# Attention scores over four rotating PSUM banks, and a ring of three banks for everything else

## What is computed

```python
s = (jnp.einsum('bqhd,bkhd->bhqk', qn_b, k_nope)
     + jnp.einsum('bqhr,bkr->bhqk', qr_b, k_rope)) * ATTN_SCALE
p = jax.nn.softmax(s.astype(jnp.float32), axis=-1).astype(v.dtype)
return jnp.einsum('bhqk,bkhd->bqhd', p, v)
```

## Time and profile before

| | |
|---|---|
| median of three executions | 1463.22 us (1460.0 to 1464.26) |
| the profiled execution | 1462.78 us |
| its span | 1460.6 us |
| TensorE busy in the span | 1377.5 us (94%) |
| attention, first score to the closing stage's first data | 183.7 to 514 us |

### The profile page before, as it was taken

How to read it: one execution, slowest core, us unless ns; L and a number is a source line. 1 busy time by engine, 2 the same in 40 slices (tenths; PEclk the granted TensorE clock), 3 DMA queues, 4 the chain that set the end, 5 groups by cost and what they waited for, 6 DMA issues and landing times.

```text
span 1460.6 us, 20549 instructions
## 1 busy us (share of the span) xinstructions
PE 1377.5 (94%) x7548; PEld 1236.6 (85%) x7548; DVE 818.7 (56%) x1206; ACT 708.7 (49%) x1416; POOL 441.9 (30%) x542
## 2 busy tenths in 40 slices
PE   5899889999999979999999999999999999999996
PEld 1599878999888858899999888899998879999995
DVE  6577577777777744245555455544445545444444
ACT  5677567787777732243333443433334433333332
POOL 3476637888778624450000001100000020000002
PEclk9899999999999989999999999999999999999999
DMA  8522001111111060053443333433333334333321
GB/s 295 168 77 78 28 17 40 42 42 42 42 37 37 25 243 1 34 219 137 160 170 129 116 115 116 159 142 115 128 130 116 116 116 159 142 115 129 130 86 43
DMA packets 50445, 154.63 MB, mean 106 GB/s; under 512 B 9832, under 2 KB 12392, under 8 KB 50376
## 3 DMA queue, kind: packets, MB, share of 16 engines
q1 hardware_dynamic: 49512, 150.60, 29.3%
q0 software_dynamic: 864, 3.15, 0.5%
HBM read 148.73 MB, written 4.83 MB: 105 GB/s over the span
## 4 chain that ended last, share of the span: by engine, by line
PE 60%; DVE 2%; POOL 1%; ACT 1%; DMA 0%; issue 0%; DVEq 0%; ACTq 0%; POOLq 0%
PE bank L2048 27%; PE bank L2040 26%; PE bank L1756 6%; POOL x L1829 1%; PE bank L1530 1%; DVE wol L1718 0%; DMA add<-in_w_o 0%; DVE w1l L1935 0%; DVE w2l L1935 0%; PE bank L1561 0%; DVE add L1979 0%; PE bank L2062 0%; ACT w2h L1866 0%; DVE rTl L1946 0%; ACT rTh L1884 0%
## 5 line engine op out<-in xcount | busy, mean ns | idle before, releaser
L2040 PE MATMUL bank<-h2h,w1l 128*128 128x384 f32 x768 | 258.2, 336 | 0.0
L2040 PE MATMUL bank<-h2l,w1h 128*128 128x384 f32 x768 | 258.2, 336 | 0.0
L2040 PE MATMUL bank<-h2h,w1h 128*128 128x384 f32 x768 | 258.2, 336 | 0.0
L1829 POOL TENSOR_TENSOR x<-x,add 128x512 f32<-128x512 f32 x16 | 20.9, 1334 | 717.8 <-DVE add L1979 717.8
L2048 PE MATMUL bank<-w2h,rTh 128*128 128x512 f32 x576 | 182.7, 398 | 7.8 <-DVE rTl L1946 7.8
L2048 PE MATMUL bank<-w2l,rTh 128*128 128x512 f32 x576 | 179.7, 393 | 0.0
L2048 PE MATMUL bank<-w2h,rTl 128*128 128x512 f32 x576 | 179.0, 392 | 0.0
L1884 ACT ACTIVATE rTh<-sq 128x384 fp32r<-128x384 f32 x94 | 49.4, 525 | 243.6 <-PE bank L2048 239.7
L1873 ACT ACTIVATE relu<-bank 128x384 f32<-128x384 f32 x94 | 46.1, 491 | 247.1 <-PE bank L2040 247.1
L1946 DVE TENSOR_TENSOR rTl<-sq,rTh 128x384 fp32r<-128x384 f32 x96 | 53.6, 558 | 174.1 <-ACT rTh L1884 169.9
L1935 DVE TENSOR_TENSOR w1l<-w1raw,w1h 128x1024 fp32r<-128x1024 f32 x94 | 117.2, 1247 | 55.2 <-ACT w1h L1866 55.2
(11 more groups left out here) (269 smaller groups left out, 2904.2 us busy)
## 6 DMA issues: line engine op xcount, KB each, us to landing
w1raw<-in_w SPq DMA_DIRECT2D x96, 512.0 KB, 3.7
w2raw<-in_w SPq DMA_DIRECT2D x96, 512.0 KB, 4.6
ada_raw<-in_w_ada SPq DMA_DIRECT2D x24, 512.0 KB, 4.8
xn<-in_w_ada SPq DMA_DIRECT2D x16, 512.0 KB, 3.5
xin<-in_x SPq DMA_DIRECT2D x9, 512.0 KB, 3.6
x<-in_x SPq DMA_DIRECT2D x3, 1536.0 KB, 12.4
g_raw<-in_w_ada SPq DMA_DIRECT2D x8, 512.0 KB, 3.5
out_y<-x POOLq DMA_DIRECT2D x6, 512.0 KB, 5.4
```

The lines of the kernel that those rows point to most:

```text
L1829: nc.gpsimd.tensor_tensor(k.x[:, t, cut], k.x[:, t, cut], add[:, i, :], ALU.add).then_inc(out_added, 1)
L2040: op = nc.tensor.matmul(bank[6 + s][:, 0:BN], w[0][s][x][:, c * P:(c + 1) * P], k.h2[b % 2][y_][:, c, :], start=n == 0, stop=n == 3 * DC - 1)
```

## The change

The scores get a fourth bank: column c of unit u is item n = 3u + c and goes to bank n % 4 of banks 0 to 3. It waits for the exponential that read item n-4. An access can't wrap from bank 3 to bank 0, so the unit's three columns are read as 2 and 1, and in units with u % 4 = 1 (columns in banks 3, 0, 1) as 1 and 2. The ring loses bank 3: item n waits for the reader of item n-3. Side products move: keys from x = 0, 3, 5 to 1, 3, 6, queries from 1, 4, 7 to 2, 5, 7. On VectorE `low_key` moves from behind `maximum(u)` to the head of the unit, ahead of the output sum and the maximum. The gate columns of unit 0 go through bank 3, and the wait for their reader moves to the start of `scores(1)`.

The items that a side or context product waits for, by unit of a head (T2 same unit means: the low half of this unit's own T2):

| x | before: item and what it waits for | after |
|---|---|---|
| 0 | k0: q2 | |
| 1 | q0: k0 | k0: T2 same unit |
| 2 | | q0: k0 |
| 3 | k1: T1 of u-1; context: T2 same unit | k1: T2 same unit; context: T3 same unit; T4: q0 |
| 4 | q1: k1 | T1: k1 |
| 5 | k2: q1; context: T2 same unit | q1: T2 same unit; context: T3 same unit |
| 6 | | T1: q1; k2: context of u-1 |
| 7 | q2: T1 of u-1; context: T2 same unit | T4: k2; q2: T2 same unit; context: T3 same unit |

```diff
--- before.py
+++ after.py
@@ -318,7 +318,7 @@
         LAST = NU + 4
         NV = LT + 2
         KCUT = ((0, 512), (512, 1024), (1024, NKEY))
-        SIDE_AT = {0: ("k", 0), 1: ("q", 0), 3: ("k", 1), 4: ("q", 1), 5: ("k", 2), 7: ("q", 2)}
+        SIDE_AT = {1: ("k", 0), 2: ("q", 0), 3: ("k", 1), 5: ("q", 1), 6: ("k", 2), 7: ("q", 2)}
         NADA = 16
         ADA0 = 3 * DC
         ADA_AT = {4 + 15 * r // 4: r for r in range(NADA)}
@@ -328,7 +328,18 @@
         KEY_ITEM, QUERY_ITEM = (2, 3, 4), (1, 5, 6)
         VALUES_FREE = {2: 6 + NV - 1, 3: 6 + NV}
         VALUES_AT = {0: range(0, 2), 1: range(2, 6), 2: range(6, NV)}
-        scores_in, pv_bank, ring_banks = k.banks[:, 0:3, 0:BN], bank[6], (bank[3], bank[4], bank[5], bank[7])
+        pv_bank, ring_banks = bank[6], (bank[4], bank[5], bank[7])
+
+        def score_parts(u):
+
+            first = 3 * u % 4
+            cut = 1 if first == 3 else 2
+            return [(first + lo) % 4 for lo in (0, cut)], ((0, cut), (cut, 3))
+
+        def score_read(n):
+
+            u, c = divmod(n, 3)
+            return 2 * u + 1 + (c >= score_parts(u)[1][0][1])
 
         def query(n, x):
 
@@ -380,11 +391,11 @@
         place = {item: n for n, item in enumerate(ring)}
 
         def ring_bank(what, i):
-            return ring_banks[place[what, i] % 4]
+            return ring_banks[place[what, i] % 3]
 
         def ring_free(pe, what, i):
 
-            n = place[what, i] - 4
+            n = place[what, i] - 3
             if n < 0:
                 return
             kind, j = ring[n]
@@ -826,8 +837,8 @@
                         act.wait_ge(rs_ready, 2 * u - 14)
                     if u >= 4:
                         act.wait_ge(t_filled, KI * ((u - 4) // 2) + KI)
-                    for part, (lo, hi) in enumerate(((0, 2), (2, 3))):
-                        nc.scalar.activation(prow[:, s, lo * BN:hi * BN].rearrange("p (a b) -> p a b", b=BN), scores_in[:, lo:hi, :],
+                    for part, (at, (lo, hi)) in enumerate(zip(*score_parts(u))):
+                        nc.scalar.activation(prow[:, s, lo * BN:hi * BN].rearrange("p (a b) -> p a b", b=BN), k.banks[:, at:at + hi - lo, 0:BN],
                                              ACT.Exp, bias=nm[:, s:s + 1], scale=SCALE,
                                              accum_out=psum[:, u % 8, part:part + 1]).then_inc(p_exp, 1)
 
@@ -1074,7 +1085,7 @@
                     at = 2 * DC
                     dve.wait_ge(cols_done, 5)
                     for j in range(2):
-                        nc.vector.tensor_tensor(k.mod[:, at:at + DC, j], bank[4][:, 0:2 * DC].rearrange("p (c j) -> p c j", j=2)[:, :, j],
+                        nc.vector.tensor_tensor(k.mod[:, at:at + DC, j], bank[3][:, 0:2 * DC].rearrange("p (c j) -> p c j", j=2)[:, :, j],
                                                 k.cols[:, C_BADA + at:C_BADA + at + DC], ALU.add).then_inc(gain_done, 1)
 
                 def turn_query(n, b, freed):
@@ -1097,9 +1108,9 @@
 
                 def maximum(u):
                     s = u % 4
-                    for part, (lo, hi) in enumerate(((0, 2), (2, 3))):
+                    for part, (at, (lo, hi)) in enumerate(zip(*score_parts(u))):
                         dve.wait_ge(s_filled, 2 * u + part + 1)
-                        nc.vector.tensor_reduce(mx[:, s, part:part + 1], scores_in[:, lo:hi, :], AX_XY, ALU.max).then_inc(nm_ready, 1)
+                        nc.vector.tensor_reduce(mx[:, s, part:part + 1], k.banks[:, at:at + hi - lo, 0:BN], AX_XY, ALU.max).then_inc(nm_ready, 1)
                     dve.wait_ge(nm_ready, 3 * u + 2)
                     nc.vector.tensor_scalar(nm[:, s:s + 1], mx[:, s, 0:1], mx[:, s, 1:2], -SCALE, ALU.max, ALU.mult).then_inc(nm_ready, 1)
 
@@ -1205,6 +1216,10 @@
                 pooled(15)
                 for u in range(LAST):
                     h, s = divmod(u, LT)
+                    side = side_of(u - 1) if u else None
+                    if side and side[0] == "k":
+                        dve.wait_ge(side_filled, side_place[side] + 1)
+                        low_key(side[1], ring_bank("k", side[1]), side_freed)
                     n = half_read(u)
                     if n is not None:
                         dve.wait_ge(out_low, n + 1)
@@ -1220,10 +1235,6 @@
                         low_value(v)
                     if u == 0:
                         gate_columns()
-                    side = side_of(u - 1) if u else None
-                    if side and side[0] == "k":
-                        dve.wait_ge(side_filled, side_place[side] + 1)
-                        low_key(side[1], ring_bank("k", side[1]), side_freed)
                     if u - 1 in MOD_AT:
                         modulation(MOD_AT[u - 1])
                     if ctx_now(u - 1, "turn"):
@@ -1322,10 +1333,9 @@
                     if cs[0] == 0:
                         pe.wait_ge(g1_lat, 2 * DC)
                         pe.wait_ge(g1_ctx, 2 * DC)
-                        pe.wait_ge(setup_freed, QUERY_ITEM[1])
                     for c in cs:
                         for j in range(2):
-                            op = nc.tensor.matmul(bank[4][:, 2 * c:2 * c + 2], g1_acc[:, c // 4, j, c % 4 * P:(c % 4 + 1) * P], k.sel[:, j, :],
+                            op = nc.tensor.matmul(bank[3][:, 2 * c:2 * c + 2], g1_acc[:, c // 4, j, c % 4 * P:(c % 4 + 1) * P], k.sel[:, j, :],
                                                   start=j == 0, stop=j == 1)
                     if cs[-1] == DC - 1:
                         op.then_inc(cols_done, 1)
@@ -1371,15 +1381,18 @@
                             pe.wait_ge(setup_freed, KEY_ITEM[2])
                         else:
                             pe.wait_ge(side_freed, side_read("k", 3 * h + 2))
+                    if u == 1:
+                        pe.wait_ge(gain_done, 6)
                     if t % BLK == 0:
                         pe.wait_ge(q_lo, 3 * h + t // BLK + 1)
                     for c in range(3):
-                        if u and c != 1:
-                            pe.wait_ge(p_exp, 2 * u - 1 + c // 2)
+                        n = 3 * u + c
+                        if n >= 4:
+                            pe.wait_ge(p_exp, score_read(n - 4))
                         for i, (x, y) in enumerate(((0, 0), (0, 1), (1, 0))):
-                            op = nc.tensor.matmul(bank[c][:, 0:BN], query(3 * h + t // BLK, x)[:, t % BLK * P:(t % BLK + 1) * P], kT[j][y][:, c * BN:(c + 1) * BN],
+                            op = nc.tensor.matmul(bank[n % 4][:, 0:BN], query(3 * h + t // BLK, x)[:, t % BLK * P:(t % BLK + 1) * P], kT[j][y][:, c * BN:(c + 1) * BN],
                                                   start=i == 0, stop=i == 2)
-                        if c:
+                        if c == 2 or c + 1 == score_parts(u)[1][0][1]:
                             op.then_inc(s_filled, 1)
 
                 def turn(i):
@@ -1501,8 +1514,6 @@
                     for i in values_of(u):
                         values(i)
                     side = side_of(u)
-                    if u == 1:
-                        pe.wait_ge(gain_done, 6)
                     if side:
                         ring_free(pe, *side)
                         if side[0] == "q":
```

## The result

The changed kernel takes 1472.12 us (median; 1471.23 to 1472.72) where the kernel before, run beside it, takes 1461.61 (1459.21 to 1464.26). The ratio is 1.0061 with an interval of 1.0040 to 1.0081: 0.6% slower, which is about 9 us by the ratio (the medians are 10.5 apart) and clear of the noise. The forecast had 1467.0 with 1455 to 1474, so the time lies in the range, but more than twice as far from the old one as the sum of +4.2 said. The profiled execution took 1472.13 us.

What follows compares the result with a forecast made beforehand. The attention's end was taken to bound the kernel. Heads 1 to 6 +3.1, head 0's second half +0.4, its opening +0.4, head 7 -1.7 and scalings +2 made +4.2: 1462.8 became 1467.0 us, range 1455 to 1474.

Steps and rivals of the forecast that it cites:

- What bounds the kernel: The closing stage starts when the attention ends, so what the attention gains or loses moves the end one for one.
- Part 1, four banks: Column 0 fills the wait for the exponential; loop 0.53 us shorter, even units 3.72, odd 4.08 or 3.8.
- Part 2, places: Side products a unit later: same work, TensorE bounds of 3.6 to 4.8 us a unit, keys and queries in time.
- rival B: Slower: ScalarE's scalings, fed by GpSimd, add in full, 8.8 in place of 2, giving 1474 us; chance 0.18.
- Parts 3 and 4, the ring and the low half: Waiting for T2, 0.3 at x = 3; early low_key adds 0.75 at x = 7; units 6 and 7: 10.27.
- Rival A: Faster: the waits for T2 in the heads are hidden; half of that gain gives 1455 us; chance 0.25.
- The scalings: ScalarE's weight scalings in eight units push the maximum or the binding chain; bounded by 0 and 10.8, taken as +2.
- Rival B's sign: Waits of VectorE on ScalarE's copy well over 22 us would show that the scalings add in full.
- Head 7's end and the opening: Head 0: second half +0.4 and first four units +0.4; units 56 to 63 together -1.7.
- +0.8 for head 0: Second half of head 0 +0.4; its first four units +0.4, bounded by 0.5 of gain and 1.7 of loss.
- the tail's -1.7: Units 56 to 62 make 28.5 plus 0.6 for scalings against 31.3; unit 63 loses 0.5; together -1.7.
- rival C: TensorE's clock falls at the stop of x = 7 in seven heads, 1.5 each, giving 1477 us; chance 0.05.

Runs made afterwards that it cites:

- e2: Changed kernel with the scores back in three banks and their old waits, ring of three and both moves kept: 1474.55 us, ratio 1.0068.
- e9: Kernel before with only the new places of the side products; three score banks, ring of four, low_key behind the maximum: 1460.50 us, ratio 0.9988.
- e3: Kernel before with the new side-product places and low_key at the unit's head, but three score banks and ring of four: 1469.04 us, ratio 1.0028.
- e5: Changed kernel with low_key back behind the maximum: 1477.15 us, ratio 1.0087.
- e8: Kernel before with ScalarE's scaling of streamed weights behind the output copy in units 39, 43, 47 and 51: 1462.58 us, ratio 1.0003.
- e4: Changed kernel with side products at x = 0, 1, 2, 4, 5, 6 from head 1 on (head 0: 1 to 6): 1468.99 us, ratio 1.0045.
- e11: Kernel before with ScalarE's scaling behind the output copy in units 39, 47 and 51, not 43: 1462.91 us, ratio 0.9991.
- e6: Changed kernel with the side products of heads 1 to 7 at their old places: 1472.70 us, ratio 1.0063.
- e10: Changed kernel with the first modulation product in unit 20 instead of unit 18: 1471.56 us, ratio 1.0050.
- e7: Changed kernel with ScalarE's scaling of streamed weights behind the output copy in units 39, 43, 47 and 51: 1472.82 us, ratio 1.0065.
- e12: Kernel before with the new side-product places and ScalarE's scaling behind the output copy in units 39, 47 and 51: 1461.83 us, ratio 0.9995.

## Why the prediction was right or wrong

**What bounds the kernel** stood. What the attention lost came through to the end, but for 1.9 of 11.5. Of the four modulation products that I counted in heads 1 to 6, one stands in unit 63, outside them; no term of the sum rests on it.

**Part 1, four banks**: the gain at x = 0 (3.7 forecast, 3.71 measured) and in units 56 to 62 (2 to 3 shorter; 2.7) was right, and column 0 starts without a wait. A unit's gain isn't the head's: e2 prices the rotation at 3.1 for heads 1 to 6, 0.5 a head. For units 6 and 7 my sum had that, since I had laid them as one chain. At x = 4 the unit took 3.7 in most heads and not 4.5, and x = 5 some 5.6 and not 4.9, as the wait stands before column 1: together 8.95 to 10.3 against 9.4.

**Part 2, places**: x = 2 4.72 (4.7), x = 3 4.65 to 5.38, and 6.16 and 5.94 behind scalings (4.95). e9 measures 1.4 for six heads, with three score banks. What I left out is the queue of ScalarE: I costed the moved side products on TensorE only, and the query's high half went with them. At x = 7 it stands ahead of the high halves and, in e9, waits for GpSimd in units 39 and 47, 1.0 us of unit length each. I wrote that GpSimd feeds the scalings (rival B), and not that it feeds this. In the kernel after it costs next to nothing: the wait is there in unit 39 only (1.29), beside the chain that binds.

**Parts 3 and 4, the ring and the low half**: the mechanism is confirmed by the rows of unit 23. The query waits 0.89 behind VectorE's low half, less than the 1.0 to 1.4 named, and units 6 and 7 take 10.53 where 10.27 was worked out. The wait of 0.3 at x = 3 didn't come as a rule: it was 0.17 in unit 11, 0.90 in units 43 and 51 behind a scaling, and none in units 19, 27 and 35. Rival A (x = 7 under 5.3) falls. But what I priced there is shared out otherwise than I thought. I gave 0.75 of x = 7 to the key's halves ahead of the maximum; from 4.92 before, e9 has 5.13, e3 5.40, e2 6.20, after 6.44, so the place makes 0.2, the early low half 0.3, the ring 0.8 and the earlier start of the unit's scores 0.25. The early low half costs at x = 4, where I had it too (release at 4.5 instead of 3.6); with the rotation that wait moves into unit 5. e5 shows that low_key's place can't be priced alone.

**The scalings**: +2 was taken between 0 and 10.8. Measured as what the eight units named are longer than the commonest length of their x, it was about 6.2 before and 7.5 after: +1.3. Of that the half clock in unit 39 is 1.1. The scaling itself makes units 39 and 47 longer by 1.2 each, where it was 0.9 before. What was too small instead is the head without scalings: the commonest lengths make 37.9 and not 37.4, so 1.0 a head and not 0.5, and 0.3 of the difference is units 6 and 7. That 5.1 stood against a measured 6.5 is partly luck, as one term was too small and the other too large. Rival B's sign (waits of VectorE on the copy well over 22 us) did not come as written, as those fell to 12.7; but the waits had moved to the key behind that copy, 24.2. I had named the wrong line for the right queue.

**Head 7's end and the opening**: here the sum failed. The +0.8 for head 0 was measured as +3.8, and the tail's -1.7 as +1.5: units 56 to 62 gave 2.7 where 2.2 was worked out, and unit 63 lost 4.2 where 0.5 was. Both have half clock in them, and the clock had no term in the sum. So that the time lies under 1474 is luck in part: that bound was made for the scalings, and something else filled it. I had given rival C 0.05 because "the rows show no fall in mid attention". The earlier trace rows themselves showed 0.72 for 214 to 220: the opening was where TensorE already lost the clock. They also show more idle at 1.00 than I wrote, 3.0 of 40 us from 422 to 462. In mid attention C came too, in one unit of 48, one of the two at x = 7 that a scaling makes longest. Unit 47, with the same scaling and the same stops to 0.02 us, stayed at full clock and took 7.65 to unit 39's 8.75, so about 1.1 is what it cost, and why the one fell and the other didn't is open. The ordinary stop at x = 7, which C multiplied by seven heads, cost nothing of the kind.

The Trainium skill, "TensorE: Matmul & The Clock Gate", section "A second HAM failure mode: psum-queue depth-cycling", describes a clock that goes up and down with short idles between groups of matmuls. By that rule the heads should have lost all along; the rows of 262 to 302 at 1.00 speak against that, while unit 39, where the stops are longer, and both ends agree with it. Unit 47, with unit 39's stops and no fall, shows that the length of the stops doesn't settle it here.

7 us more at half clock in the opening can cost 3.5, nearly all of the 3.8. But head 0 is the same code in before and e8, and took 50.78 with 7 us at half clock and 53.36 with 10: more than the clock alone can make, so something else differs there, and no run tells what. Kernels that differ in head 0 only by edits of this kind had 0 us (e9), 7 (before, e4, e11), 10 (e2, e3, e5, e6, e8, e10) and 14 (after, e7, e12), and head 0 took 47.5, 50.3 to 50.8, 51.8 to 53.6 and 53.1 to 54.6. At the same clock the change thus costs head 0 nothing that shows.

Does the change make the falls likelier, or was the clock of the profiled execution chance? The mean granted clock of a whole execution is on record for all of them, not only for the profiled ones. The kernel before, in 87 executions beside the experiments, had a median of 0.984, and 17 of the 87 were at 0.981 or less. The kernel after had all four there (0.979 to 0.981), and e6, e7 and e10, which leave its banks and its ring as they are, 18 of 20. So the lower clock comes with the change, and is not chance alone. The 17 executions of before took 1466.05 in the median (1464.23 to 1469.81). Against these the change costs 6 us, against the one at 0.979 (1468.06) 4; the other 4 to 6 of the 10.5 come with the clock. This doesn't show in which stage the clock was lost.

**The sum, mended** for the profiled execution: start -0.3; head 0 +3.8, up to 3.5 of it clock; heads 1 to 6 +6.5; units 56 to 62 -2.7; from unit 63 on +4.2, of which the clock 2.6 and the rest 1.5, about 1 of it the context product's wait (it starts 4.75 into the unit, 3.71 before); closing stage -1.9. That is 9.6. In the heads, from before over e9, e3 and e2 to after: places +1.4, low half early +6.0, ring +2.3, rotation -3.1, together 6.6 for the 6.5. These steps hold in this order only: e5 shows that the second has the other sign once the third is in. The medians differ by 10.5, which is 0.9 more; executions of one kernel lie several us apart (before from 1458.47 to 1469.81), so that last us has no cause of its own that I could show.

## What to carry to other kernels

When a product moves in a schedule, follow each thing it drags along into the in-order queue of every engine: with the new places alone the query's high half moved too, waited for GpSimd, and in two units held up the high halves and the exponential behind it by 1.0 us. Work put ahead of a reduction on the engine that frees banks is paid in every unit where the next product needs a freed bank; moving the product elsewhere moves the wait with it. Ask of the clock at the places where it is already low in the profile before, in the last unit, and in the unit with the longest stop, not in a stretch's mean. And compare executions of two kernels at like mean clock before you give all of a difference to the schedule.

## What the runs showed of the hardware

TensorE waited 0.89 at the query of unit 23, and of units 7, 15 and 31 too, and from 222 to 390 us the clock stayed at 1.00; with 1.9 idle of 4 us in unit 39 it fell to 0.52, and with the same stops in unit 47 it stayed at 1.00. In unit 63, with 0.83 idle ahead of the context product and then matmuls of two columns, it fell to 0.54; with four filler matmuls it was 1.00. The stop isn't needed for that: in e9 and e11 unit 63 has none ahead of the context product, and had 3.4 us at half clock behind the matmuls of two columns. The opening had between 0 and 14 us at half clock in nearly the same code (PEclk of 180 to 230: 1.00 in e9, 0.93 before, 0.90 in e8, 0.86 after). In the kernel before an execution's time follows its mean granted clock: 18 executions at 0.986 or more took 1460.5 in the median, 17 at 0.981 or less 1466.05. A score matmul of 384 columns takes 0.34 at the one level and 0.69 at the other, as in the opening of after:

```profile
194.01 0.69 PE L1393 MATMUL bank<-kTh,qh 128*128 128x384 f32 x1 [0.33 <-DVE mod L1088]
```
